# Masks, waits and one more convolution block moved between the engines of a two-model kernel

## The chip, the cores and the metric

One core of a Trainium2 chip runs the whole program. Times are device microseconds (us) of that core. Its engines are TensorE (PE in the rows; its weight loads are PEld), VectorE (DVE), ScalarE (ACT), GpSimd (POOL) and SyncE (SP), which issues the DMAs. Each takes its instructions in order and waits on semaphores.

## What is computed

Two small transformers run one after the other on 256 tokens of width 1024, batch 1, in float32. Cut to what matters here:

```python
# block 1, layer 0: convolution module; layer 1: forgetting attention over 12 heads
def conformer_conv(u, b_glu, w_dw, b_dw, ln_g, ln_b):
    a, gate = jnp.split(u + b_glu, 2, axis=-1)
    v = a * jax.nn.sigmoid(gate)
    v = causal_dwconv(v, w_dw, b_dw)          # 31 taps, 768 channels, one filter a channel
    return jax.nn.silu(layernorm(v, ln_g, ln_b))
# both layers: 4 heads of attention to a memory, then
x = x + jnp.concatenate([mix, mem_o], axis=-1) @ w_out[l]
x = x + conv_ffn(rmsnorm(x, g_ffn[l]), w_up[l], w_dw_f[l], b_dw_f[l], w_down[l])

# block 2, layer 1: sparse attention, 16 heads; for each of the two blocks of 128 queries
p_c = softmax over 16 compressed keys, p_s over selected keys, p_w over a window
return gates[..., 0:1] * o_c + gates[..., 1:2] * o_s + gates[..., 2:3] * o_w
```

With 256 tokens there are four selection blocks, and all are selected, so p_s and p_w are both causal attention over the keys, with different keys.

## The kernel before, in words

**Weights.** They come as 173 tiles of 1 MB (`TILES`), always in the same order. SP loads tile t into one of three slots of `RAW`, after VectorE is through with tile t-3. ScalarE rounds it to `WH` (line 1318), VectorE subtracts and writes the rest to `WL` (line 1687), and TensorE takes three products for each pair: high by high, low by high, high by low (lines 792 to 794). ScalarE may round tile t only when TensorE has used tile t-3 (`w_used`). On ScalarE and VectorE the place of these two instructions in the queue is written by hand: `upto(key)` or `upto_n(n)` rounds (or splits) all tiles up to n+2 that are not done yet.

**The convolution** works on six blocks of 128 channels. Four (`PE_BLOCKS` = 2, 3, 4, 5) are matmuls on TensorE (line 944): the sequence is copied by DMA into four shifted copies (`shift(j)` on SP, 16 DMAs each, for a pair of blocks), and the taps are diagonal matrices of 32 by 32, which GpSimd builds from `pick` and the tap values (line 724). Blocks 0 and 1 are done on VectorE, 31 taps each, one instruction a tap (lines 1880 and 1882), in turn, spread over the program by `taps(count)`. TensorE's blocks lie in the slots of the first memory attention (`CONV_SLOTS`). The mean for the layer norm (line 1090) needs all six.

**Attention** runs as a pipeline of slots. In slot s TensorE takes a piece of a weight tile, the scores of head s, the transposes of head s-2 and, for every second slot, the product with the values. VectorE takes the maximum (line 1793), ScalarE the exponential (line 1403), VectorE normalizes (line 1779) and copies the transposes (line 1801). In the second attention (12 heads and 4 memory heads, `base` 4) `FOX_PIECES` says which tile's half goes to which slot; slot 11 ends `("qm", 1)`, whose bank VectorE empties with `by_head` (line 1758), and slots 12 to 16 hold halves of `("o1", c)`.

**The FFN** runs 11 steps (`ffn`); step s has the tiles fg and fv, and from step 2 (`LAG`) also fd of step s-2. ScalarE does the middle tap (line 1424), the tanh (line 1428, which waits for VectorE) and the high part of the product (line 1433); VectorE does the scaling (line 1748), two taps (lines 1830, 1834) and the low part.

**A normalized input** is transposed by TensorE (line 926), and ScalarE writes the high parts from the bank (line 1351), VectorE the low parts (line 1716). Norm 3 has two gains, hence two targets: `KH`/`KL` (in MH/ML) first needed by tile `("k1", 0)`, and `XH`/`XL`.

**The sparse attention** has 16 heads, one in a slot. In slot s TensorE computes the scores of head s into two banks, `Ss` and `Sw` (lines 1262 to 1269), then the transposes of head s-1 (lines 1275, 1276), one whole tile of queries or gates (48 matmuls), and the values of head s-1 (lines 1290 to 1293). Masks are added on TensorE: matmuls of an identity in bf16 with the masks `causb` and `cmpb`. VectorE takes five maxima from the banks (lines 2250 to 2254); ScalarE reads the banks again for the six exponentials (line 1652), copies a transposed part (lines 1662, 1663) and then rounds the next tile; VectorE normalizes (line 2282) and splits the tile.

## Time and profile before

| | |
|---|---|
| median of 3 runs | 1224.46 us (1223.63 to 1225.26) |
| the profiled execution | 1224.42 us |
| its span, first to last instruction | 1222.6 us |
| PE busy | 1176.3 us, 96% of the span |
| DVE busy | 854.8 us, 70% |
| ACT busy | 599.6 us, 49% |
| mean granted TensorE clock | 0.990 |

Busy PE is the time in which a matmul is in flight, so it hides what a matmul costs; the spacing of starts shows that. A wait row names an engine's first instruction behind the wait and who released it. The granted clock is 1.0 at 2.4 GHz and 0.5 at 1.2 GHz.

### The profile page before, as it was taken

Reading aid. Unit: us, or ns where it says so; the run is one execution under the profiler, and the core shown is the slowest. Engines: PE = TensorE matmul, PEld = TensorE weight load, DVE = VectorE, ACT = ScalarE, POOL = GpSimd, SP = SyncE. Lnnn points to the kernel's source line nnn. Section 1 sums busy time; section 2 is a strip of 40 time slices with the busy share of each in tenths; the row PEclk is TensorE's granted clock in tenths of the full one; section 3 lists DMA queues with packets and bytes.
Section 4 is the critical chain, followed back from the end, with each engine's and each line's share of the span. In section 5 each row is a group of like instructions: output and inputs, shape, how many; then the busy total and the mean of one; then the engine's idle time right before and its main releaser. Section 6 shows DMA issues by size and latency. Waiting matters only on the chain.

```text
span 1222.6 us, 19215 instructions
## 1 busy us (share of the span) xinstructions
PE 1176.3 (96%) x7966; PEld 1054.6 (86%) x7966; DVE 854.8 (70%) x1310; ACT 599.6 (49%) x933; POOL 24.6 (2%) x40
## 2 busy tenths in 40 slices
PE   6989998999999999899999999999999999999997
PEld 6958898999899779899999978878799789999885
DVE  5995678787767657887778856665676257777664
ACT  6525545545554435455545334444553245565552
POOL 3000000000000000000000000000000000000000
PEclk9999999999999999999999999999999999999998
DMA  9634444555443314455544544544575522322351
GB/s 378 209 108 158 173 173 174 199 179 179 183 173 118 125 69 173 140 205 177 198 176 152 208 158 149 203 156 155 206 276 207 211 99 99 106 103 104 136 192 50
DMA packets 31398, 202.81 MB, mean 166 GB/s; under 512 B 4048, under 2 KB 4176, under 8 KB 8784
## 3 DMA queue, kind: packets, MB, share of 16 engines
q1 hardware_dynamic: 31312, 201.58, 45.3%
q8 instruction: 63, 1.03, 0.3%
q14 instruction: 23, 0.19, 0.0%
HBM read 198.18 MB, written 1.05 MB: 163 GB/s over the span
## 4 chain that ended last, share of the span: by engine, by line
PE 82%; DVE 9%; ACT 4%; issue 2%; DMA 1%; DVEq 0%; ACTq 0%; POOLq 0%; SPq 0%; POOL 0%
PE bank L792 24%; PE bank L793 23%; PE bank L794 23%; DVE WL L1687 3%; ACT WH L1318 2%; DVE work L1882 2%; PE bank L1292 1%; PE bank L1275 1%; PE bank L1218 1%; PE bank L1182 1%; PE bank L926 1%; PE bank L1006 1%; DMA xn<-cmpw 1%; PE bank L1266 1%; DVE work L1834 1%
## 5 line engine op out<-in xcount | busy, mean ns | idle before, releaser
L1687 DVE TENSOR_TENSOR WL<-RAW,WH 128x2048 fp32r<-128x2048 f32 x172 | 394.8, 2298 | 154.4 <-ACT WH L1318 153.2
L1318 ACT ACTIVATE WH<-RAW 128x2048 fp32r<-128x2048 f32 x172 | 328.5, 1912 | 215.5 <-PE bank L794 207.6
L792 PE MATMUL bank<-XH,WH 128*128 128x256 f32 x1264 | 363.1, 287 | 19.5 <-DVE WL L1903 11.9
L793 PE MATMUL bank<-XL,WH 128*128 128x256 f32 x1264 | 359.5, 284 | 0.0
L794 PE MATMUL bank<-XH,WL 128*128 128x256 f32 x1264 | 359.4, 284 | 0.0
L792 PEld LDWEIGHTS bank<-XH,WH 128*128 128x128 f32 x1264 | 244.4, 193 | 23.6 <-DVE XL L1896 11.8
L793 PEld LDWEIGHTS bank<-XL,WH 128*128 128x128 f32 x1264 | 244.5, 193 | 0.6
L794 PEld LDWEIGHTS bank<-XH,WL 128*128 128x128 f32 x1264 | 244.3, 193 | 0.0
L792 PE MATMUL bank<-WH,MH 128*128 128x512 f32 (+1 forms) x480 | 182.3, 380 | 3.7 <-DVE work L1758 2.7
L793 PE MATMUL bank<-WL,MH 128*128 128x512 f32 (+1 forms) x480 | 179.9, 375 | 0.0
L794 PE MATMUL bank<-WH,ML 128*128 128x512 f32 (+1 forms) x480 | 179.5, 374 | 0.0
L792 PEld LDWEIGHTS bank<-WH,MH 128*128 128x128 f32 x480 | 91.1, 190 | 20.9 <-DVE work L1758 2.9
L794 PEld LDWEIGHTS bank<-WH,ML 128*128 128x128 f32 x480 | 91.2, 190 | 16.2
L793 PEld LDWEIGHTS bank<-WL,MH 128*128 128x128 f32 x480 | 91.3, 190 | 14.7 <-issue 0.2
L792 PE MATMUL bank<-WH,XH 128*128 128x512 f32 x192 | 76.3, 397 | 0.0
L794 PE MATMUL bank<-WH,XL 128*128 128x512 f32 x192 | 74.8, 389 | 0.0
L793 PE MATMUL bank<-WL,XH 128*128 128x512 f32 x192 | 74.7, 389 | 0.0
L792 PE MATMUL bank<-MH,WH 128*128 128x256 f32 x208 | 60.2, 289 | 5.9 <-DVE ML L1716 2.9
L793 PE MATMUL bank<-ML,WH 128*128 128x256 f32 x208 | 58.8, 283 | 0.0
L794 PE MATMUL bank<-MH,WL 128*128 128x256 f32 x208 | 58.8, 283 | 0.0
L1652 ACT ACTIVATE work<-bank,stat,rs_n 128x128 f32<-128x128 f32 (+2 forms) x96 | 43.0, 463 | 23.7 <-DVE stat L2256 23.7
L1424 ACT ACTIVATE work<-work,par 128x256 f32<-128x256 f32 x88 | 47.5, 588 | 6.3 <-DVE work L1748 6.3
(294 smaller groups left out, 1471.3 us busy)
## 6 DMA issues: line engine op xcount, KB each, us to landing
RAW<-wstream SPq DMA_DIRECT2D x173, 1024.0 KB, 4.8
con<-cmpw SPq DMA_DIRECT2D x6, 512.0 KB, 5.7
xn<-cmpw SPq DMA_DIRECT2D x4, 512.0 KB, 7.6
con<-consts SPq DMA_DIRECT2D x1, 1617.0 KB, 6.7
work<-xT_in SPq DMA_DIRECT2D x1, 1024.0 KB, 4.9
x<-x_in SPq DMA_DIRECT2D x1, 1024.0 KB, 10.8
work<-mem_in SPq DMA_DIRECT2D x1, 1024.0 KB, 15.8
xn<-memT_in SPq DMA_DIRECT2D x1, 1024.0 KB, 13.2
```

The lines of the kernel that those rows point to most:

```text
L792: mm(o, ah, bh, start=start, stop=False)
L793: mm(o, ah, bl, start=False, stop=False)
L794: return mm(o, al, bh, start=False, stop=stop)
L926: last = nc.tensor.transpose(o[j][:, kk * T + i * P:kk * T + (i + 1) * P], x[:, i, (2 * j + kk) * P:(2 * j + kk + 1) * P], ident)
L1006: mm(o[:, a:a + n], q1[h % 2][:, h // 2, t], k1[:, h // 2, 0:n], start=True, stop=False)
L1182: last = mm(o[:, :], sdt[:, h % 2, a:a + P], rv[:, m, :], start=(m == 0), stop=(m == i))
L1218: last = mm(o_cmp[r, 0:256], blocks[:, l, r], cmp_w[n % 2][2 * v + i // 4][:, c], start=(n == 0 and i == 0), stop=(n == 3 and i == 7))
L1318: act_fn(WH[:, t % RING, :], RAW[:, t % RING, :], ACT.Copy).then_inc(w_rounded, 1)
L1424: act_fn(fy[:, e, c], fu[:, e, c], ACT.Identity, bias=col(f"b_dw_f{l}", f), scale=col(f"w_dw_f{l}", 2 * 44 + f)).then_inc(act_for_dve, 1)
L1652: ins = act_fn((pC, pS, pW)[dst][:, e, b:b + w], B((name, s))[:, a:a + w], ACT.Exp, bias=stat[:, c:c + 1], scale=rs_n[:, i:i + 1], accum_o ...
L1687: tt(WL[:, t % RING, :], RAW[:, t % RING, :], WH[:, t % RING, :].bitcast(F32), ALU.subtract).then_inc(w_split, 1)
L1882: link(stt(conv[:, b, :], vpad[:, b, i - 1:i - 1 + T], tap(b, i - 1), conv[:, b, :], ALU.mult, ALU.add))
```

## The change

Six things at once.

- **FFN.** For the first two steps both engines had one tile more in their `upto_n` (the term `0 < 2 * s + q < 2 * LAG`). It is gone. ScalarE now rounds one tile before the tanh in steps 0, 1 and 2.
- **Second attention.** `by_head(("qm", 1), ...)` moves on VectorE from the end of slot 11 to ahead of that slot's maximum; VectorE's `upto` in slot 16 is left out there and comes behind the loop.
- **Norm 3.** ScalarE and VectorE do both pairs of the first gain before the second gain. ScalarE waits for VectorE's low part of a pair before it reads the bank for the second gain.
- **Sparse slots.** No mask matmuls. The key array is laid out anew, so that four score matmuls (144, 272, 256 and 128 columns) do what four of 256, 256, 272 and 16 did. VectorE adds the masks and takes the maxima in one instruction a segment, six in a slot, each followed by a read of the accumulator, and writes the masked scores to SBUF; ScalarE takes the exponentials there. The banks `Ss` and `Sw` are freed by VectorE. Tiles are rounded and split a slot earlier. ScalarE's copy of the transposed part comes ahead of its exponentials. From slot 13 on VectorE's `output` comes at the end of a slot for the head before.
- **Convolution.** Block 1 goes to TensorE too; VectorE keeps block 0, with half as many taps at each place.
- **Tap matrices and shifts.** The diagonal matrices come from DRAM ready made (512 KB a block, 5 DMAs behind the loads of tiles 5 to 8) and GpSimd builds none. Each group of 16 shift DMAs stands behind one more weight load than before, and there is a third, shorter group for block 1.

```diff
-PE_BLOCKS = (2, 3, 4, 5)
+PE_BLOCKS = (2, 3, 1, 4, 5)
-CONV_SLOTS = {0: [(2, 0), (2, 1)], 1: [(3, 0)], 2: [(3, 1)], 3: [(4, 0)], 4: [(4, 1)], 5: [(5, 0)], 6: [(5, 1)]}
+CONV_SLOTS = {0: [(2, 0), (2, 1)], 1: [(3, 0)], 2: [(3, 1), (1, 0)], 3: [(1, 1)], 4: [(4, 0), (4, 1)], 5: [(5, 0)], 6: [(5, 1)]}
+TAPS_AFTER = {5: (2, 3), 6: (1,), 7: (4,), 8: (5,)}
...
-                if TILES[t] == ("mk", 1):
+                if TILES[t] == ("mv", 1):
                     shift(1)
                 if TILES[t] == ("o0", O0_ORDER[0]):
+                    shift(0)
+                if TILES[t] == ("o0", O0_ORDER[1]):
                     sp.wait_ge(w_used, TILE[("qm", 0)] + 1)
                     shift(2)
...
                 load(t)
+                for b in TAPS_AFTER.get(t, ()):
+                    if t == 5:
+                        sp.wait_ge(front_lo, KD)
+                    sp.dma_start(conv_w[b], tapw[b].rearrange("p (n c) -> p n c", c=DIAG)).then_inc(conv_w_loaded[b], 16)
...
-            conv_weights(2)
-            conv_weights(3)
-            conv_weights(4)
             rms(0)
-            conv_weights(5)
...
-                    mm(oS[:, 0:T], q0, k[:, P:P + T], start=True, stop=False)
-                    mm(oS[:, 0:T], identb[:, :], causb[:, :], start=False, stop=True)
-                    mm(oS[:, T:2 * T], q1_, k[:, 0:T], start=True, stop=False)
-                    mm(oS[:, T:T + P], identb[:, :], causb[:, 0:P], start=False, stop=True).then_inc(aux_done, 1)
-                    mm(oW[:, 0:T + CMP_S], q1_, k[:, T:KALL], start=True, stop=False)
-                    mm(oW[:, P:T], identb[:, :], causb[:, 0:P], start=False, stop=False)
-                    mm(oW[:, T + CMP_S:T + 2 * CMP_S], q0, k[:, 2 * T:KALL], start=False, stop=False)
-                    mm(oW[:, T:T + 2 * CMP_S], identb[:, :], cmpb[:, :], start=False, stop=True).then_inc(aux_done, 1)
+                    at = P + CMP_S
+                    mm(oS[:, 0:at], q0, k[:, P:T + CMP_S], start=True, stop=False)
+                    mm(oS[:, at:at + T + CMP_S], q1_, k[:, 0:T + CMP_S], start=False, stop=True).then_inc(aux_done, 1)
+                    mm(oW[:, 0:T], q1_, k[:, KEYS_WIN], start=True, stop=False)
+                    mm(oW[:, T:T + P], q0, k[:, at + P:at + 2 * P], start=False, stop=True).then_inc(aux_done, 1)
...
-                for j in (2 * h, 2 * h + 1):
-                    ready(act, ("tr", n, j))
-                    for dst, _, name in [norms[n][g] for g in gains]:
+                for at, (dst, _, name) in enumerate([norms[n][g] for g in gains]):
+                    for j in (2 * h, 2 * h + 1):
+                        ready(act, ("tr", n, j))
+                        if at:
+                            act.wait_ge(part_done, j + 1)
...
-                        upto_n(at + 1 + q + (0 < 2 * s + q < 2 * LAG))
+                        upto_n(at + 1 + q)
...
                         if q == 0:
+                            if s <= LAG:
+                                upto_n(at + 2)
                             act.wait_ge(*dve_a.next())
...
-                    if s in pieces:
+                    if s in pieces and s < n:
                         upto(pieces[s][0])
+                    if s in pieces and pieces[s] == (("qm", 1), 1):
+                        by_head(("qm", 1), q_mem)
...
-                    link(nc.vector.tensor_reduce(m3[:, 1:3, 0], oS[:, 0:T].rearrange("p (b k) -> p b k", b=2), AX_X, ALU.max))
-                    link(nc.vector.tensor_reduce(mx[:, 3:4], oS[:, T:2 * T], AX_X, ALU.max))
-                    link(nc.vector.tensor_reduce(mx[:, 0:1], oW[:, T + CMP_S:T + 2 * CMP_S], AX_X, ALU.max))
-                    link(nc.vector.tensor_reduce(mx[:, 1:2], oW[:, T:T + CMP_S], AX_X, ALU.max))
-                    link(nc.vector.tensor_reduce(mx[:, 5:6], oW[:, 0:T], AX_X, ALU.max))
+                    for br, i, dst, b, w, name, a, mask in NSA_SEGMENTS:
+                        ins = nc.vector.tensor_tensor_reduce((pC, pS, pW)[dst][:, e, b:b + w], B((name, s))[:, a:a + w], mask, 1.0, -3e38,
+                                                             ALU.add, ALU.max, mx[:, 2 * br + i:2 * br + i + 1])
```

**ScalarE in the third step of an FFN.** Before, from the high part of step 1 to the first tap of step 2's second half:

```order
L1433 ACTIVATE MH<-work 128x512 [waits dve_for_act]
L1424 ACTIVATE work<-work,par 128x256 [waits freed_A_dve]
L1424 ACTIVATE work<-work,par 128x256
L1428 ACTIVATE work<-work 128x512 [waits dve_for_act]
L1318 ACTIVATE WH<-RAW 128x2048 [waits w_used,w_loaded2]
```

Now (line 1430 was 1433, 1311 was 1318, 1425 was 1428):

```order
L1430 ACTIVATE MH<-work 128x512 [waits dve_for_act]
L1311 ACTIVATE WH<-RAW 128x2048 [waits w_used,w_loaded1]
L1419 ACTIVATE work<-work,par 128x256 [waits freed_A_dve]
L1419 ACTIVATE work<-work,par 128x256
L1311 ACTIVATE WH<-RAW 128x2048 [waits w_used,w_loaded2]
L1425 ACTIVATE work<-work 128x512 [waits dve_for_act]
```

The tile of slot 2 (fv of step 3) is rounded ahead of the tanh and its wait for VectorE, and the tile of slot 1 came to stand in this step instead of the one before.

**TensorE and VectorE in a slot of the sparse attention.** Before, TensorE's scores with the first transpose behind them, and VectorE's maxima with the output ahead of them:

```order
L1262 MATMUL bank<-work 128x256 [waits freed_A_act,freed_B_act]
L1263 MATMUL bank<-causb,identb 128x256
L1264 MATMUL bank<-work 128x256
L1265 MATMUL bank<-causb,identb 128x128
L1266 MATMUL bank<-work 128x272
L1267 MATMUL bank<-causb,identb 128x128
L1268 MATMUL bank<-work 128x16
L1269 MATMUL bank<-cmpb,identb 128x32
L1275 MATMUL bank<-ident,work 128x128 [waits prob_done,freed_A_dve,freed_A_act]
```

```order
L2241 SCALAR_TENSOR_TENSOR xn<-bank,work 128x256 [waits aux_done]
L2250 TENSOR_REDUCE stat<-bank 128x2 [waits freed_B_dve,aux_done]
L2251 TENSOR_REDUCE stat<-bank 128x1
L2252 TENSOR_REDUCE stat<-bank 128x1
L2253 TENSOR_REDUCE stat<-bank 128x1
L2254 TENSOR_REDUCE stat<-bank 128x1
L2256 SCALAR_TENSOR_TENSOR stat<-stat,rs_n 128x6 [waits dve_chain]
```

Now the same on TensorE, and the first rows on VectorE (ISA is the fused instruction, ISA stat the read of its accumulator):

```order
L1259 MATMUL bank<-work 128x144 [waits freed_A_act,freed_B_dve]
L1260 MATMUL bank<-work 128x272
L1261 MATMUL bank<-work 128x256
L1262 MATMUL bank<-work 128x128
L1268 MATMUL bank<-ident,work 128x128 [waits prob_done,freed_A_dve,freed_A_act]
```

```order
L2234 SCALAR_TENSOR_TENSOR xn<-bank,work 128x256 [waits aux_done]
L2249 ISA work,stat<-bank,con 128x128 [waits freed_B_dve,aux_done]
L2249 ISA stat 128x1
L2249 ISA work,stat<-bank,con 128x16
L2249 ISA stat 128x1
L2249 ISA work,stat<-bank,con 128x256
```

Four matmuls left TensorE's slot, and five instructions of VectorE became twelve (six pairs).

**SP's queue around the shifts.** Before, where the first 16 shift DMAs begin, and now:

```order
L642 DMA xn<-memT_in 128x2048
L619 DMA RAW<-wstream 128x2048 [waits w_split] x5
L627 DMA MH<-work 32x572 [waits glu_done]
```

```order
L682 DMA work<-tapw 128x1024 [waits front_lo]
L682 DMA gfree<-tapw 128x1024 [waits front_lo]
L626 DMA RAW<-wstream 128x2048 [waits w_split]
L682 DMA con<-tapw 128x1024
L626 DMA RAW<-wstream 128x2048 [waits w_split]
L682 DMA con<-tapw 128x1024
L626 DMA RAW<-wstream 128x2048 [waits w_split]
L682 DMA con<-tapw 128x1024
L626 DMA RAW<-wstream 128x2048 [waits w_split]
L638 DMA MH<-work 32x572 [waits glu_done]
```

Tile 9 is loaded ahead of the shifts instead of behind them, and five tap matrices stand between the loads of tiles 5 to 9.

## Rows read from the trace of the kernel before

**Rows 1.** The page, busy time of the engines with instruction counts:

```profile
PE 1176.3 (96%) x7966; PEld 1054.6 (86%) x7966; DVE 854.8 (70%) x1310; ACT 599.6 (49%) x933; POOL 24.6 (2%) x40
```

**Rows 2.** TensorE's waits, whole run: line, releaser, total us, times, longest:

```profile
PE bank L792 <- DVE WL L1687: 8.8, 6, 3.3
PE bank L1017 <- DVEq L1802: 3.9, 2, 2.6
PE bank L792 <- DVE ML L1716: 2.9, 3, 1.5
PE bank L792 <- DVE work L1758: 2.7, 1, 2.7
PE bank L1275 <- DVE work L2282: 1.0, 1, 1.0
```

**Rows 3.** Busy time by stretch, last columns: clock, DMA share, GB/s:

```profile
90.00:93.40 3.40, 2.93 (x20) 1.42 (x24) 2.92 (x8) 3.23 (x7) 0.00 (x0) 0.51 0.00 0
...
192.40:195.80 3.40, 3.40 (x30) 3.40 (x30) 3.40 (x4) 2.43 (x3) 0.00 (x0) 0.99 0.36 113
...
509.90:513.30 3.40, 3.31 (x15) 3.35 (x16) 3.33 (x7) 0.79 (x2) 0.00 (x0) 0.50 0.67 236
```

**Rows 4.** Timeline, first FFN, third step: start, us, engine, instruction, idle before:

```profile
184.12 0.63 ACT L1428 ACTIVATE work<-work 128x512 f32<-128x512 f32 x1 [1.98 <-DVEq L1837]
184.66 1.90 ACT L1318 ACTIVATE WH<-RAW 128x2048 fp32r<-128x2048 f32 x1
...
186.59 2.29 DVE L1687 TENSOR_TENSOR WL<-RAW,WH 128x2048 fp32r<-128x2048 f32 x1 [1.72 <-ACT WH L1318]
```

**Rows 5.** Timeline, end of the second attention, VectorE and TensorE:

```profile
420.13 0.47 PE L792 MATMUL bank<-WH,MH 128*128 128x512 f32 x1 [2.69 <-DVE work L1758]
...
443.13 2.29 DVE L1687 TENSOR_TENSOR WL<-RAW,WH 128x2048 fp32r<-128x2048 f32 x1 [0.98 <-ACT WH L1318]
...
447.33 0.44 PE L1017 MATMUL bank<-work,mvv 128*64 128x256 f32 x2 [2.57 <-DVEq L1802]
```

**Rows 6.** TensorE's waits from 20 to 130 us:

```profile
PE bank L792 <- issue: 2.1, 1, 2.1
PE bank L979 <- DVE work L1779: 2.0, 2, 1.2
PE bank L1017 <- DVEq L1802: 1.4, 1, 1.4
PE bank L792 <- DVE WL L1687: 1.3, 2, 1.0
```

**Rows 7.** The chain that ended last, half a convolution block; then VectorE's taps, timeline:

```profile
95.40 1.86 PE bank L944 x32
...
57.27 3.26 DVE L1882 SCALAR_TENSOR_TENSOR work<-work,par 128x256 f32<-128x256 f32 x8
```

**Rows 8.** Timeline, TensorE in one sparse slot: first score, mask, transpose, next slot:

```profile
1006.24 0.60 PE L1262 MATMUL bank<-work 128*128 128x256 f32 x2
1006.68 0.27 PE L1263 MATMUL bank<-causb,identb 128*128 128x256 bf16 x1
...
1008.07 0.31 PE L1275 MATMUL bank<-ident,work 128*128 128x128 f32 x1
...
1016.48 0.38 PE L1262 MATMUL bank<-work 128*128 128x256 f32 x1
```

**Rows 9.** Groups of VectorE, 1006 to 1120 us: count, busy, mean ns, idle before:

```profile
L1687 DVE TENSOR_TENSOR WL<-RAW,WH 128x2048 fp32r<-128x2048 f32 x12 | 27.5, 2292 | 7.1 <-ACT WH L1318 7.1
...
L2250 DVE TENSOR_REDUCE stat<-bank 128x2 f32<-128x256 f32 x11 | 4.7, 426 | 7.9 <-PE bank L1269 7.9
...
L2252 DVE TENSOR_REDUCE stat<-bank 128x1 f32<-128x16 f32 x11 | 1.8, 165 | 0.0
```

**Rows 10.** Timeline, VectorE in one sparse slot: bias, then behind the exponentials:

```profile
1030.00 0.17 DVE L2256 SCALAR_TENSOR_TENSOR stat<-stat,rs_n 128x6 f32<-128x6 f32 x1
...
1033.01 0.19 DVE L2271 RECIPROCAL stat<-stat 128x6 f32<-128x6 f32 x1 [1.14 <-ACT work L1652]
```

More of the change, by code:

```diff
@@ L1709, in low @@
             def low(n, h, gains=(0,)):
-                for j in (2 * h, 2 * h + 1):
-                    dve.wait_ge(*hi_a.next(2 * len(gains)))
-                    for g in gains:
-                        hi, dst, name = norms[n][g]
+                for g in gains:
+                    hi, dst, name = norms[n][g]
+                    for j in (2 * h, 2 * h + 1):
+                        dve.wait_ge(*hi_a.next(2))
                         for kk in range(2):
@@ L1863, in ple @@
                         low(8, 0)
-            TAPS_IN_SLOT = 4
-            dve_taps = [(b, i) for i in range(CONV) for b in (0, 1)]
+            TAPS_IN_SLOT = 2
+            dve_taps = [(0, i) for i in range(CONV)]
             n_tap, last_of, glu_at = [0], {}, {}
@@ L1934, in _ @@
                             .then_inc(front_lo, 1)
-                taps(6 if j < 2 else 8)
+                taps(3)
             dve.wait_ge(mask_made, 1)
@@ L1938, in _ @@
             upto(("qm", 0))
-            taps(10)
+            taps(5)
             spread(0)
@@ L1942, in _ @@
             upto(("mk", 0))
-            taps(8)
+            taps(6)
             upto(("mv", 0))
@@ L2229, in gate_in, with output @@
                 scaled(("ng", t), nu.rearrange("p (b t) -> p b t", b=2))
+            upto(("ng", 0))
             gate_in(0)
             gate(0)
-            upto(("ng", 0))
+            EARLY_OUT = NSA_H - 3
+            def output(h):
+                e = h % 2
+                ready(dve, ("On", h))
+                free(stt(om[:, e, :], B(("On", h))[:, 0:T], 0.5, gs[:, (h // 2) % 2, e * T:e * T + T], ALU.mult, ALU.mult),
+                     ("On", h), "dve")
+                is_free(dve, ("On", h))
+                dve.drain().then_inc(dve_for_act, 1)
@@ L2234, in _ @@
             for s in range(NSA_H + 2):
                 e = s % 2
[L2236 to L2244 removed]
+                if 2 <= s <= EARLY_OUT:
+                    output(s - 2)
@@ L2392, in param_array, with conv_tap_matrices @@
     return np.ascontiguousarray(np.concatenate([v[n] for n, _ in PARAM_PARTS], axis=1))
-def conv_taps_by_shift(w):
-    out = np.zeros((SHIFTS * STEPS, 4 * P), np.float32)
-    out[0:CONV] = w[:, 2 * P:]
-    return out.reshape(STEPS, SHIFTS, 4, GROUPS, DIAG).transpose(1, 4, 2, 3, 0).reshape(P, 4 * GROUPS * STEPS)
+def conv_tap_matrices(w):
+    taps = np.zeros((SHIFTS * STEPS, MIX), np.float32)
+    taps[0:CONV] = w
+    taps = taps.reshape(STEPS, SHIFTS, NMB, GROUPS, DIAG).transpose(2, 1, 4, 3, 0).reshape(NMB, P, GROUPS * STEPS)
+    out = np.zeros((NMB, P, GROUPS * STEPS, DIAG), np.float32)
+    for r in range(P):
+        out[:, r, :, r % DIAG] = taps[:, r]
+    return out.reshape(NMB, P, GROUPS * STEPS * DIAG)
 def channels(v):
```

147 lines of the change are left out of this document (69 added, 78 removed).

## Prediction

> **What bounds the kernel now.** I read the page's busy times first: a matmul is in flight for 96% of the span [rows 1]. That share says only that TensorE is the engine to watch, not that it runs at its peak, so the second view is its waits [rows 2]: few and short, some 23 us beside the start of the run, which nothing here touches [rows 2, 6]. They come in clusters: two of 3.3 us in the FFNs, 2.7 and 2.6 at the end of the second attention, and 6.8 in four entries in the convolution [rows 2, 6]. The third view is the granted clock by stretch [rows 3]. Behind five of the waits it is at 0.5 (1.2 GHz) for 3.4 us: from 90.0, 189.0, 421.1, 448.4 and 509.9; rows 3 show the first and the last. In such a stretch TensorE starts 15 or 16 matmuls of a gemm, in the next one of the same length 30. So each costs another 3.4 / 2 = 1.7 us, and removing a wait of 3 us pays 5. Everywhere else TensorE runs back to back, and there only fewer or shorter matmuls help. The sparse slots are such a place: of rows 2 only the 1.0 us lies there, in the second slot, and from then on it is VectorE that waits for TensorE, by 7.9 / 11 = 0.7 us a slot [rows 9].
>
> **FFN, both of them.** The wait of 3.3 us is for the low part of tile fv of step 3 [rows 2]. The split begins at 186.59, after VectorE stood 1.72 us for ScalarE, whose rounding ran at 184.66 because it is queued behind the tanh of 184.12, itself held 1.98 us by VectorE [rows 4]. ScalarE did not wait for TensorE or a load before it, so data and slot were there. It is a knot of two queues and no shortage. The change puts the rounding ahead of the tanh: it would run in the 1.98 us idle from 182.1, ready at 184.0. That alone moves the split 2.6 us. The same 1.72 us wait stood in each of the two steps before, and the surplus tile of step 0 kept VectorE a whole split, 2.3 us, from its taps, so VectorE also arrives earlier. Laid out instruction by instruction with the durations of rows 4 (rounding 1.90, split 2.29), I get the split done at about 182 instead of 188.9. TensorE wants it at 188.9 - 3.3 = 185.6: a margin of some 3.5 us. The tile before it (fg of step 3) is the next to be late: split done near 177.4, wanted a tile earlier, at about 179.8 (48 matmuls at 0.12 us), a margin of 2.3. Next in line is therefore TensorE itself. Gain 3.3 + 1.7 = 5.0 each, 10.0 for both; if the margins were all wrong, 0, if half a wait stays and the clock still falls, 3.
>
> **Second attention.** The 2.69 us at 420.13 are for `by_head` of tile qm [rows 5], since `("o1", 0)` needs its bank. In the new place VectorE starts it about when TensorE ends that tile, and it is out 0.3 us after TensorE wants the bank. What is queued behind it is the maximum of slot 11, late by some 0.5 us; nobody waits, for the probabilities of slot 11 are wanted two slots later. Gain 2.4 + 1.7. The 2.57 us at 447.33 come behind a split of 2.29 us that VectorE did ahead of the copy [rows 5]. Without it the copy starts when the transpose is there, and 0.68 + 0.2 us of copy and drain stay: gain 1.7 + 1.7. The split then comes behind the loop; its tile is wanted some 8 us later, so it is free. Together 7.5; bounds 4 (clock falls all the same) and 8.5.
>
> **Norm 3.** TensorE waits 2.9 us in three places for line 1716 [rows 2], the longest (1.5) at norm 8, which keeps its order, the other 1.4 at tile ("k1", 0). With the first gain done first, VectorE's low part starts two ScalarE instructions (0.7 us) earlier and the second pair follows at once. Gain 1.3, at least 0.5. ScalarE's new wait for VectorE is about 0.2 us per pair, under TensorE's transposes.
>
> **Convolution.** Removed from VectorE: 31 taps of block 1. In the rows a tap of alternating blocks costs 3.26 / 8 = 0.4 us [rows 7]. With one block each tap waits for the one before; I take 0.5. So VectorE does 31 x 0.5 = 16 us where it did 62 x 0.4 = 25: 9 us less before 98 us, where its taps stood ahead of the scaling and splits that TensorE waited for. Added on TensorE: a block is two halves of 1.86 us [rows 7], 3.7 us on the path. Tile 9's load no longer stands behind 16 shift DMAs. Played through, the waits of 6.8 us and one half-clock stretch (1.5) go, as VectorE is 2 to 4 us early at each: 6.8 + 1.5 - 3.7 = 4.6, of which I take 4.5. In my laying out of SP's queue the shifts for block 4 leave by 75 us and are wanted at 82, those for block 1 by 64 and are wanted at 76. The tap matrices are 2.6 MB more, half a megabyte beside each megabyte tile. At one tile in 5.7 us that is 184 + 92 = 276 GB/s; 236 GB/s made the DMA engines 0.67 busy [rows 3], so they fit. GpSimd's building is off every path. Bounds: 6, and -2 if half the waits stay and 3.7 is paid.
>
> **Sparse slots.** The first matmul of a slot to the next slot's is 1016.48 - 1006.24 = 10.24 us, and scores with masks take 1008.07 - 1006.24 = 1.83 [rows 8]. A score of 256 columns takes 0.44 [rows 8]. Before and after there are 800 columns of scores, so without masks they take at best 800 / 256 x 0.44 = 1.38: gain 0.45. At the least it is what the masks' 544 columns cost at the gemm's pace of 3.4 us / 30 for 256 columns [rows 3]: 0.24. I take 0.40, because the two 16-column pieces, costly for their size, vanish into wider ones. 16 slots: 6.4; bounds 3.8 and 7.2. TensorE's 1.0 us wait for line 2282 in slot 1 [rows 2] goes as well, since the rounding and split of the tile move ahead of slot 0. Sum 7.4.
>
> This holds only if VectorE's loop fits into 9.84 us. Before it took 10.24 - 0.72 = 9.52 [rows 8, 9]. The columns are again 800. Added are one instruction and six reads of an accumulator, which no row of VectorE shows. The nearest are its 16-column maxima, spaced 0.08, and ScalarE's read of its accumulator at 0.2: seven short instructions are 0.6 to 1.4 us. The exponentials (3.0 us, [rows 10]) read SBUF instead of a bank; from 0.0 to 0.3. The 7.1 / 12 = 0.6 us wait for ScalarE's rounding [rows 9] goes, as its copy no longer stands in front. 9.52 + 0.6 + 0.1 - 0.6 = 9.6 fits; with the high ends 10.6 does not. I take the low one, since spacing on the same engine is the nearer row. A little over would not hurt either: by the same laying out the probabilities are ready about 2.5 us before TensorE wants them, so a loop 0.2 us too long is used up only after 12 slots.
>
> **Sum.** 10.0 + 7.5 + 1.3 + 4.5 + 7.4 = 30.7. The profiled execution took 1224.42 us with a span of 1222.6; the median is 1224.46, so what lies around the span stays 1.8 and the same sum holds for both: 1224.46 - 30.7 = 1193.8.
>
> **Rivals.**
> *The slot becomes VectorE's.* If the accumulator reads cost 0.2, the loop is 10.2 to 10.6; after the 2.5 us of reserve the slots run at that pace, 0.0 to 0.4 over the old one for some eight of them. The sparse gain falls from 7.4 to between 0 and 4: 1197 to 1201. Against it: short instructions on VectorE are spaced 0.08.
> *The fused instruction runs at half pace.* It has a bank and SBUF as sources and an accumulator. At two cycles a column the 800 columns add 800 / 256 x 0.33 = 1.0 us: a loop of 10.6 from the third slot on, sparse -5 instead of +7.4: about 1206. Against it: a tap, which reads two f32 tensors from SBUF without an accumulator, keeps 0.4 us for 256 columns [rows 7]. The Trainium skill, "Vector Engine (DVE) Microarchitecture Reference", section "Points that are easy to get wrong", says that this family of instructions halves its throughput with two non-bf16 SBUF sources, since no port is left for the accumulator. By its letter a bank as one source escapes it, and the taps of this trace don't show it; if it applied here too, the time would be this rival's.
> *The queues knot again elsewhere.* One of the FFN margins (2.3 us) or of the attention's is wrong by more than itself, and as the code is the same in both FFNs it costs twice: 6 to 10 us less gain, 1199 to 1204.
> *The convolution does not pay.* Shifts or VectorE's chain in the memory attention hold TensorE, and 3.7 us are paid for nothing: 1198 to 1200.
> *Slower than before.* Only the fused instruction can do it: with 23 us gained elsewhere, 13 slots would each have to be 1.9 us longer than 10.24, a loop of 12.1. That needs 0.7 us for each of the six pairs on average, where I count 0.3: an instruction that falls off its normal path, as one without a name of its own in this list could. About 1230.
>
> **Chances.** Forecast 0.55, VectorE's slot 0.13, half pace 0.06, a knot 0.10, convolution 0.07, slower 0.03, more gain than the sum (down to 1187, all upper bounds) 0.06. The range 1187 to 1203 takes in all but the last cases of half pace, knot and slower. A change within 0.2% (2.4 us), which is about what a measurement can tell, would need one case to eat exactly the rest: 0.01. Faster 0.96.
>
> **What would show it.** Right: TensorE's waits in both FFNs' third steps gone and no stretch at 0.5 before the last microseconds; scores from first matmul to transpose in 1.4 us and slots of 9.84; the last half block of the convolution (95.4 before, [rows 7]) at about 91; line 1716's wait at k1 about 0.1. Wrong: TensorE waiting in the sparse slots for the normalization on VectorE (rival one or two, told apart by the spacing of the fused instructions: 0.35 or 0.6 for 256 columns, and by that of the reads), waits for shifts or tap matrices at line 944, or a gap in the FFN that moved to another tile.

## The result, and the profile after

The changed kernel takes 1193.95 us (median of four runs, 1192.96 to 1194.86), the kernel before 1224.86 us in the same measurement: a ratio of 0.975, 95% interval 0.973 to 0.977. The prediction was 1193.8. It hit, but as a sum whose terms erred in both directions; where each erred is shown below. The profiled execution took 1194.86 us with a span of 1193.1.

The page after, busy time of the engines:

```profile
PE 1163.9 (98%) x7966; PEld 1049.0 (88%) x7966; DVE 842.8 (71%) x1392; ACT 604.9 (51%) x934; POOL 14.2 (1%) x33
```

TensorE's waits after, whole run (line, releaser: total us, times, longest); they answer to [rows 2]:

```profile
PE bank L789 <- DVE WL L1897: 12.2, 1, 12.2
PE bank L789 <- DVE ML L1710: 1.5, 1, 1.5
PE bank L789 <- issue: 1.1, 1, 1.1
PE bank L1013 <- DVEq L1798: 1.0, 1, 1.0
PE bank L789 <- DVE WL L1681: 1.0, 2, 0.7
PE bank L1214 <- DMA xn<-cmpw: 0.9, 1, 0.9
PE bank L789 <- DVE work L1752: 0.6, 1, 0.6
```

The first is the start of the run; the one of 1.1 us, to which the profile gives no releaser ("issue"), stands in norm 3 and is taken up below. Of the 8.8 us for splits 1.0 is left, and both FFNs and the whole convolution have no wait at all. Busy time by stretch, in the places where the clock had fallen or would fall (us, busy and instructions of PE, PEld, DVE, ACT, POOL; clock, DMA share, GB/s); it answers to [rows 3]:

```profile
90.00:93.40 3.40, 3.40 (x55) 1.75 (x48) 1.77 (x2) 0.00 (x0) 0.00 (x0) 1.00 0.00 0
177.00:180.40 3.40, 3.40 (x31) 3.40 (x30) 3.37 (x6) 2.17 (x2) 0.00 (x0) 1.00 0.48 142
408.50:411.90 3.40, 3.13 (x14) 2.67 (x15) 1.79 (x7) 2.72 (x5) 0.00 (x0) 1.00 0.00 0
433.00:436.40 3.40, 3.40 (x19) 2.52 (x18) 2.00 (x2) 0.39 (x1) 0.00 (x0) 1.00 0.00 0
```

All at 1.0, and the trace records no fall of the clock between 18.3 and 1189.0 us; the kernel before had five. The two spans differ by 29.5 us. Read at the same instruction in both traces, they part as in the table. The instructions are TensorE's: the first spreading of a norm (the matmuls with `rstd` at line 839 before, 836 now), then the first transposes of norms 2, 3, 4 and 6, the first sparse score, and the first transposes of the last norm.

| stretch | lead gained, us | predicted |
|---|---|---|
| start, to the first spreading (21.93 before, 23.56 after) | -1.6 | 0 |
| convolution, to norm 2 | 5.6 | 4.5 |
| first FFN, to norm 3 | 5.0 | 5.0 |
| norm 3, to its spreading | 0.45 | 1.3 |
| second attention, to norm 4 | 6.7 | 7.5 |
| second FFN | 4.9 | 5.0 |
| block 2 up to the sparse scores | -0.5 | 0 |
| sparse slots | 9.0 | 7.4 |

The medians differ by 30.9: this execution was the slowest of its four, 0.9 us over their median, and the profiled one before was 0.4 under its own. The first line of the table is taken up at the end.

### The profile page after: what moved, and what is told of

It reads as the page before. It is cut to its first block, busy times and chain, and to the rows that moved or that the text cites. A ratio compares the mean times of both kernels' runs of the same rounds, so it can differ in the third digit from the quotient of the medians.

```text
span 1193.1 us, 19344 instructions
## 1 busy us (share of the span) xinstructions
PE 1163.9 (98%) x7966; PEld 1049.0 (88%) x7966; DVE 842.8 (71%) x1392; ACT 604.9 (51%) x934; POOL 14.2 (1%) x33
## 4 chain that ended last, share of the span: by engine, by line
PE 93%; DVE 3%; ACT 1%; DMA 1%; issue 1%; SPq 0%; DVEq 0%; POOLq 0%; POOL 0%; ACTq 0%
PE bank L789 27%; PE bank L790 26%; PE bank L791 26%; PE bank L940 2%; PE bank L1285 1%; DVE WL L1681 1%; PE bank L1214 1%; PE bank L1178 1%; PE bank L923 1%; PE bank L1268 1%; DMA xn<-cmpw 1%; PE bank L994 1%; PE bank L1002 1%; PE bank L1260 1%; PE bank L975 1%
## 5 line engine op out<-in xcount | busy, mean ns | idle before, releaser
L1657 ACT ACTIVATE work<-work,stat,rs_n 128x128 f32<-128x128 f32 (+1 forms) x96 | 46.6, 487 | 14.4 <-DVE stat L2258 14.4
L1742 DVE TENSOR_TENSOR work<-bank,rb 128x512 f32<-128x512 f32 x59 | 40.7, 689 | 12.4 <-PE bank L791 9.1
```

Source lines behind the costliest of these rows:

```text
L1657: ins = act_fn(score, score, ACT.Exp, bias=stat[:, c:c + 1], scale=rs_n[:, i:i + 1], accum_out=stat[:, 16 + c:17 + c])
L1742: ins = tt(dst, src, rbb, ALU.mult)
```

## Experiments: each part undone alone

Each run below is the changed kernel with one part put back as it was, or in two cases a piece of one. Together the five whole parts cost 29.2 us when undone one at a time (10.1, 4.9, 0.4, 4.2 and 9.6), close to the 30.9 of the change, so the parts depend little on each other.

**The FFN part.**

```diff
-                        upto_n(at + 1 + q)
+                        upto_n(at + 1 + q + (0 < 2 * s + q < 2 * LAG))
...
-                            if s <= LAG:
-                                upto_n(at + 2)
```

> The changed kernel with the FFN part alone undone: both engines have their surplus tile in the first two steps again, and ScalarE rounds no tile ahead of the tanh. Theory A (the parts add up, and the half clock behind a wait belongs to its price): TensorE waits 3.3 us again in the third step of each FFN, with a stretch at a granted clock of 0.5 behind it, and each FFN is 5.0 us longer; 1193.95 + 9.9 = 1203.9. Rival B (the clock fell in the kernel before because of what lay around the waits, not because of this wait): only 3.3 us each, 1200.6, and no stretch at 0.5. Rival C (in the new kernel VectorE reaches the FFN earlier, so part of the wait is gone anyway): under 3 us each, below 1200.

Measured: 1204.03 us, 10.1 more than the changed kernel. TensorE waits 3.26 us at 184.76 and 3.25 at 498.59, and behind the first of them:

```profile
184.70:188.10 3.40, 3.34 (x17) 3.38 (x18) 3.33 (x7) 0.79 (x2) 0.00 (x0) 0.58 0.62 222
```

Theory A. The mean clock of this window is 0.58, because the half-clock stretch starts half a microsecond into it (185.2 to 188.6). In it 15 spacings stand at 0.213 us instead of 0.12, which is 1.4 us. The second wait has such a stretch from 499.3 on. All four executions had a mean clock of 0.993 or 0.994 (0.997 or 0.998 in the changed kernel), so behind these waits it fell in all four.

**Half of the FFN part.** The surplus tile stays away, but nothing is rounded ahead of the tanh.

```diff
-                            if s <= LAG:
-                                upto_n(at + 2)
```

> The changed kernel with half of the FFN part undone: the surplus tile stays away, but ScalarE rounds no tile ahead of the tanh. The prediction gave the rounding ahead of the tanh 2.6 us of the 6.9 by which the split moved. Theory A (the knot is the rounding queued behind the tanh): the split of the tile fv in step 3 comes some 2.6 us or more later than in the changed kernel, the wait is back, and as no tile is rounded early at all, other tiles of the first steps are late too; 1203 or more. Rival B (the surplus tile made the delay by holding VectorE from its taps for 2.3 us): without it the order of rounding and tanh doesn't matter, 1194 to 1195.

Measured: 1198.57 us, 4.6 more: neither theory. TensorE's waits in the first FFN, then two stretches of it:

```profile
PE bank L789 <- DVE WL L1679: 2.0, 2, 1.4
```

```profile
176.00:179.40 3.40, 3.38 (x28) 3.40 (x29) 2.23 (x5) 1.74 (x2) 0.00 (x0) 1.00 0.60 241
179.40:182.80 3.40, 2.83 (x24) 2.66 (x23) 2.68 (x2) 3.40 (x4) 0.00 (x0) 1.00 0.16 67
```

Undoing the early rounding costs 2.4 us an FFN, and putting the surplus tile back on top of that another 2.6 (the run before). No run has the surplus tile together with the early rounding, so this split of the gain holds for this order only. Without the surplus tile the wait of 3.3 is down to 1.4 and 0.6 us, and behind 1.4 the clock stays at 1.0, in both FFNs. The stage from norm 2 to norm 3 is 2.43 us longer for listed waits of 1.98: a wait costs about 0.2 us more than its row says. A matmul is in flight for 0.28 us and starts every 0.12, and the row counts from the end of the flight, which explains 0.16 of it.

**The second attention.**

```diff
-                    if s in pieces and s < n:
+                    if s in pieces:
                         upto(pieces[s][0])
-                    if s in pieces and pieces[s] == (("qm", 1), 1):
-                        by_head(("qm", 1), q_mem)
...
+                        elif name == "qm":
+                            by_head((name, j), q_mem)
```

> The changed kernel with the part on the second attention alone undone: by_head for tile qm at the end of slot 11, and VectorE's split ahead of the copy in slot 16. Theory A: TensorE waits 2.7 us for by_head and 2.6 for the copy, as before, each with a stretch at a granted clock of 0.5 behind it; by the stages of the two traces 6.7 us, 1200.6. Rival B (the second FFN takes some of it back, since VectorE comes to it earlier or later): the wait in the attention returns in full, but the end moves by less than 5 us.

Measured: 1198.83 us, 4.9 more, the four executions from 1197.77 to 1200.28. In the profiled one, the slowest, both waits are back (2.70 and 2.57) and the attention is 6.6 us longer. Behind them:

```profile
410.20:413.60 3.40, 3.34 (x9) 2.72 (x10) 2.64 (x3) 0.43 (x1) 0.00 (x0) 0.55 0.00 0
437.60:441.00 3.40, 3.40 (x13) 2.04 (x10) 0.43 (x1) 0.38 (x1) 0.00 (x0) 0.57 0.56 236
```

The mean clock was 0.994 in this execution and 0.997, 0.996 and 0.997 in the other three; 0.997 is too high for two stretches. The waits alone make 3.6 us (1197.6), with both stretches 6.6 (1200.5): the same two waits, 2.6 and 2.7 us in the profiled execution, drop the clock twice in one execution and at most once in another. In the kernel before it was 0.989 to 0.991 in every execution on record. So the 1.7 us that the prediction gave each of these two waits were there in that kernel, but are no property of the waits alone.

**Norm 3.**

```diff
-                for g in gains:
-                    hi, dst, name = norms[n][g]
-                    for j in (2 * h, 2 * h + 1):
-                        dve.wait_ge(*hi_a.next(2))
+                for j in (2 * h, 2 * h + 1):
+                    dve.wait_ge(*hi_a.next(2 * len(gains)))
+                    for g in gains:
+                        hi, dst, name = norms[n][g]
```

(and the same in ScalarE's `high`)

> The changed kernel with the part on norm 3 alone undone. Theory A (read off the two traces: 1.24 us gained at the first half of the norm, 0.79 given back at the second, where TensorE now waits for VectorE's split of the next tile): the waits of 0.85 and 0.53 us for the low part return, the one of 1.09 behind the second transposes shrinks to 0.33, and the time is 0.45 us longer, 1194.4, which only the trace can tell. Rival B (the prediction's figure of 1.3 was right and the 1.09 us wait has another origin, such as the earlier arrival of the stage): 1195.3, and the wait of 1.09 stays.

Measured: 1194.38 us, 0.4 more, which is less than the runs of one kernel differ, so the trace decides. It has two waits of 0.85 and 0.53 us for the low part and one of 0.33 behind the second transposes. Theory A. The stretch from the first transposes to the spreading is 14.18 us, and 13.73 in the changed kernel.

**The convolution.** The whole part back, from the number of blocks to GpSimd's tap matrices:

```diff
-PE_BLOCKS = (2, 3, 1, 4, 5)
+PE_BLOCKS = (2, 3, 4, 5)
...
-            TAPS_IN_SLOT = 2
-            dve_taps = [(0, i) for i in range(CONV)]
+            TAPS_IN_SLOT = 4
+            dve_taps = [(b, i) for i in range(CONV) for b in (0, 1)]
```

> The changed kernel with the convolution part alone undone: four blocks on TensorE, two on VectorE, tap matrices built by GpSimd, shifts where they were. Theory A: waits of 6.7 us in the convolution and one stretch at a granted clock of 0.5 return, and two half blocks of 1.86 us leave TensorE; by the stages of the two traces, counted from the first spreading of a norm, 5.6 us, 1199.5. Rival B (what the trace puts down to the convolution is partly the start of the run, where the first matmuls ran at half pace for 6 us in one profile and for 3 in the other): 4 us, 1198.

Measured: 1198.14 us, 4.2 more; three executions at 1198.0 to 1198.2, the profiled one at 1199.9. TensorE's waits there, from 20 to 130 us:

```profile
PE bank L797 <- issue: 2.1, 1, 2.1
PE bank L984 <- DVE work L1782: 1.7, 2, 1.2
PE bank L1022 <- DVEq L1807: 1.4, 1, 1.4
```

Behind the 2.1 us at 57.6 the clock is at 0.5 for 3.4 us, which it was not in the kernel before behind the same wait; a second stretch, from 91.8, stands where the kernel before had its one. From the first spreading to norm 2 it takes 114.2 us, and 108.4 in the changed kernel: 5.8, of which the stretch at 57.6 is about 1.5. Theory A for the trace, B's figure for the median. The mean clock was 0.997 in two of the three faster executions and 0.996 in the profiled one, which fits one stretch less in those two; only the slowest has a trace, so this is not shown.

**Only the place of the shifts.** Five blocks on TensorE, but two groups of shifts a weight load earlier.

```diff
-                if TILES[t] == ("mv", 1):
+                if TILES[t] == ("mk", 1):
                     shift(1)
...
                     shift(0)
-                if TILES[t] == ("o0", O0_ORDER[1]):
```

> The changed kernel with the shift DMAs of blocks 2 and 3 and of blocks 4 and 5 one weight load earlier again, all else as changed (five blocks on TensorE, tap matrices from DRAM). Theory A (the wait of 2.07 us at 56.73 in the kernel before came from SP's queue: tile 9's load stood behind 16 shift DMAs, which wait for the gated values): a wait of 1 to 2 us is back near 56 us, and the time is 1 to 2.5 us longer, 1195 to 1196.5. Rival B (it came from VectorE's taps, of which only half are left): nothing returns, 1194.

Measured: 1193.39 us, no wait of TensorE from 20 to 130 us, and again 108.4 us from the first spreading to norm 2. Rival B: the place of the shifts does nothing for the time here. What removed the waits is then among the things that the run before put back together: VectorE's taps, the block on TensorE and GpSimd's matrices. The traces point to the taps. Before, six of them (48.50, 2.46 us) stand ahead of the scaling that ScalarE waits for, and the split that TensorE needs ends at 56.6; in the changed kernel three stand there (47.78, 1.52 us) and the split ends at 55.0. No run has the taps apart from the rest.

**The sparse slots.** All of that part back, here its core:

```diff
-                    mm(oS[:, 0:at], q0, k[:, P:T + CMP_S], start=True, stop=False)
+                    mm(oS[:, 0:T], q0, k[:, P:P + T], start=True, stop=False)
+                    mm(oS[:, 0:T], identb[:, :], causb[:, :], start=False, stop=True)
...
-                    for br, i, dst, b, w, name, a, mask in NSA_SEGMENTS:
-                        ins = nc.vector.tensor_tensor_reduce(...)
+                    link(nc.vector.tensor_reduce(mx[:, 3:4], oS[:, T:2 * T], AX_X, ALU.max))
```

> The changed kernel with the sparse part alone undone: masks by matmul, maxima from the banks, exponentials from the banks, tiles split a slot later. Theory A: slots of 10.24 us instead of 9.73, 16 of them, and the wait of 1.0 us in slot 1: 9.0 us by the stages of the two traces, 1203.0. The prediction had 7.4, 1201.4. What tells them apart is the spacing of slots, 0.51 or 0.40 longer.

Measured: 1203.57 us, 9.6 more; slots of 10.23 us where the changed kernel has 9.73, and the wait of 1.0 us in slot 1 is back. Theory A.

## Experiments: what a sparse slot costs

**The masks alone, on top.**

```diff
                     mm(oS[:, 0:at], q0, k[:, P:T + CMP_S], start=True, stop=False)
+                    mm(oS[:, 0:P], identb[:, :], causb[:, 0:P], start=False, stop=False)
```

(one such matmul behind each of the four scores)

> The changed kernel with four mask matmuls in bf16 put back on TensorE in each sparse slot, one behind each score (4 x 128 = 512 columns), beside the masks that VectorE adds; the mask is thus added twice, which changes no probability. It prices the masks alone, without the narrow pieces of the old layout. Theory A (they cost the 0.24 us that their spacing shows and nothing more): slots of 9.97, 16 x 0.24 = 3.8 us, 1197.8. Theory B (each change between bf16 and float32 costs the matmul behind it some 0.02 to 0.06 on top, which the 272 column score at 0.52 before and 0.46 now hints at): slots of 10.03 to 10.1, 4.8 to 6 us, 1198.8 to 1200. Rival C: the slot is already VectorE's, and TensorE's surplus is hidden: under 1196.

Measured: 1198.96 us, 5.0 more, slots of 10.11: 0.39 us a slot, and 5.9 us for the sparse stage in the traces. The changed kernel's scores first, then this kernel's (start, us, engine, line, operation); the spacing of the starts is what a matmul costs:

```profile
983.53 0.41 PE L1259 MATMUL bank<-work 128*128 128x144 f32 x2
983.78 0.62 PE L1260 MATMUL bank<-work 128*128 128x272 f32 x2
984.24 0.59 PE L1261 MATMUL bank<-work 128*128 128x256 f32 x2
984.67 0.38 PE L1262 MATMUL bank<-work 128*128 128x128 f32 x2
984.89 0.49 PE L1268 MATMUL bank<-ident,work 128*128 128x128 f32 x3
```

```profile
983.57 0.65 PE L1263 MATMUL bank<-work 128*128 128x256 f32 x2
984.05 0.22 PE L1264 MATMUL bank<-causb,identb 128*128 128x128 bf16 x1
984.11 0.44 PE L1265 MATMUL bank<-work 128*128 128x128 f32 x2
984.39 0.22 PE L1266 MATMUL bank<-causb,identb 128*128 128x128 bf16 x1
984.44 0.50 PE L1272 MATMUL bank<-ident,work 128*128 128x128 f32 x3
```

A mask takes 0.055 us, but the 128 column score behind one takes 0.28 where it takes 0.22 alone, and the 256 column score 0.48 instead of 0.43. Four masks are 0.22 us by their own rows and 0.39 by the slot. That is theory B's figure, but not its reason. In the kernel before, one mask has 256 columns and the others fewer:

```profile
1006.78 0.60 PE L1264 MATMUL bank<-work 128*128 128x256 f32 x2
1007.22 0.22 PE L1265 MATMUL bank<-causb,identb 128*128 128x128 bf16 x1
1007.22 0.30 PEld L1266 LDWEIGHTS bank<-work 128*128 128x128 f32 x2
1007.27 0.68 PE L1266 MATMUL bank<-work 128*128 128x272 f32 x2
1007.79 0.22 PE L1267 MATMUL bank<-causb,identb 128*128 128x128 bf16 x1
```

The score at 1006.78 stands behind the 256 column mask in bf16 and takes its usual 0.44; the one at 1007.27 stands behind the 128 column mask and takes 0.52, where the changed kernel's of 272 columns takes 0.46. The type changes in both places, so the change of type isn't the reason. What fits these rows is the weight load: two float32 loads in a row start 0.11 us apart (two of 0.19 us fill 0.30 in the row of L1266), a mask of 256 columns lasts as long (0.109), and one of 128 columns (0.055) leaves the other half of it open. This is read from the rows; no run was made for it.

**One more instruction on VectorE in each slot.**

```diff
                 if s < NSA_H:
+                    for c in range(1):
+                        link(stt(junk[:, c * T:(c + 1) * T], x[:, 0, 0:T], 1.0, x[:, 0, T:2 * T], ALU.mult, ALU.add))
```

> The changed kernel with one more instruction on VectorE at the head of each sparse slot: a scaled addition of two 256 column pieces of SBUF, some 0.33 to 0.4 us, whose result nobody reads. VectorE's pace in the changed kernel, from the growth of its reserve (1.33 us at head 1 to 2.27 at head 13 while TensorE's slot is 9.73): 9.65 us. Its idle time of some 1.7 us a slot, for the exponentials, lies within that loop. Theory A (VectorE's own loop is the next bound, 0.08 behind TensorE): loop 10.0, the reserve of 1.3 us is gone after four to five slots, then TensorE waits and slots are 10.0: 14 x 0.3 - 1.3 = 2.5 to 3.5 us, 1196.5 to 1197.5. Rival B (the 1.7 us of idle time absorb it): nothing, 1194. The prediction's reserve of 2.5 us would give 1 to 2 us.

**Two of them**, `range(2)`.

> The same with two such instructions, 0.66 to 0.8 us a slot. Theory A: a loop of 10.3 to 10.4 us, the reserve gone after two slots, 15 x 0.65 - 1 = 8 to 9 us, 1202 to 1203. Rival B (idle time absorbs it): 1194. It also says what the rivals of the prediction would have cost, where the fused instructions or the reads of the accumulator had been slower by that much.

Measured: 1195.65 and 1200.9 us, 1.7 and 6.9 more. VectorE's period, from the first fused instruction of a slot to that of the next, mean of an even and an odd slot, is 9.61 us in the changed kernel, 9.84 with one and 10.17 with two; TensorE's slot without waits is 9.73. The reserve (from the probabilities being ready to TensorE's transpose, us) at heads 0, 1, 6 and 12 is 0.33, 1.33, 1.7 and 2.03 in the changed kernel; 0.47, 1.12, 0.37 and 0.15 with one; 0.24, 0.57, 0.15 and 0.15 with two, where 0.15 means that TensorE waits. Theory A, with 0.23 us more for the first instruction and 0.33 for the second, where two of them are spaced 0.34. The changed kernel has 0.28 us of idle time a slot ahead of the fused instructions, which can hide a part of the first. VectorE is still idle for the exponentials. The rows are of 1002 to 1100 us, ten slots (count, busy, mean ns, idle before), in the changed kernel, then with two more instructions:

```profile
L2249 DVE CUSTOM_DVE_ANT_0 work<-bank,con 128x128 f32<-128x128 f32 (+2 forms) x60 | 13.9, 293 | 2.8 <-DVE xn L2234 1.5 <-PE bank L1269 1.3
L2273 DVE RECIPROCAL stat<-stat 128x6 f32<-128x6 f32 x10 | 1.9, 192 | 17.2 <-ACT work L1657 17.2
```

```profile
L2275 DVE RECIPROCAL stat<-stat 128x6 f32<-128x6 f32 x10 | 1.9, 191 | 16.9 <-ACT work L1657 16.9
```

The 17.2 us remain 16.9 while the slots get longer: that idle time lies inside the loop (fused instruction, exponentials, normalization, split) and absorbs nothing. With two more instructions VectorE is the bound, though it is busy for 79.1 of the 98 us only, 81%.

## Experiments: two gains that were left

**Matmuls ahead of the first tile.**

```diff
+            pe.wait_ge(mask_made, 1)
+            for _ in range(34):
+                mm(bank[7][:, 0:P], ones, ones, start=True, stop=True)
             o = take(("ca", 0))
```

> The changed kernel with 34 matmuls of 128 columns in float32 on TensorE ahead of the first tile, over a constant tile, into a bank that is first used later; nobody reads them. In the ten profiles so far the first matmuls of the run ran at half pace for 2.8 to 5.8 us (spacing 0.213 us instead of 0.12), which costs 1.4 to 2.9 us, and differs from execution to execution of one kernel. Theory A (TensorE starts at the low level of its clock because it did nothing for 12 us): the half pace falls into the idle time before the first tile; gain 1.4 to 2.9 us, 1191.0 to 1192.5, and the spread of the runs (1.9 us over four) gets smaller. Rival B (what holds the first matmuls back is tied to the first tile: loads of weights, or the other engines' start): no gain.

Measured: 1191.81 us, 2.1 less, with a spread of 0.9 instead of 1.9. From 14.9 to 18.3 us in the changed kernel, then here:

```profile
14.90:18.30 3.40, 3.40 (x18) 3.40 (x18) 2.27 (x2) 3.40 (x9) 0.71 (x1) 1.00 1.00 401
```

```profile
14.90:18.30 3.40, 3.40 (x31) 3.40 (x30) 2.03 (x2) 3.40 (x9) 0.70 (x1) 1.00 0.99 397
```

18 matmuls against 31. The view prints a granted clock of 1.00 in both, but only because the trace has no record of the clock that early: its first one, a rise to full speed, comes at 18.25 us in the changed kernel and at 5.88 here. The spacing of 0.213 us ends there too, in the changed kernel at 18.3. Theory A.

**The same, and norm 3's split earlier.** Only where a norm has two gains, VectorE's `add(acc, 3)` and `upto(key)` go between the first and the second gain:

```diff
                 for g in gains:
+                    if g and between:
+                        between()
                     hi, dst, name = norms[n][g]
```

> The same warm-up, and at norm 3 VectorE's last addition to the residual and its split of the next tile moved from behind the second gain's low part to ahead of it. Theory A (TensorE's 1.09 us wait behind the second transposes is for that split, which stands behind four low parts and an addition): the wait goes, 0.8 to 1.0 us, and the low part of the second gain is still in time; 0.9 us less than with the warm-up alone. Rival B (the second gain's low part, now 2.9 us later, is late instead): the wait moves to the tile q1 and nothing is gained. The trace tells, since 0.9 us is hardly more than the runs differ.

Measured: 1190.32 us (1189.74 to 1190.39), ratio 0.972, 95% interval 0.970 to 0.973, 3.6 less than the changed kernel: the fastest version here. VectorE at norm 3 in the changed kernel (the split ends at 329.08, and TensorE goes on at 329.18 after its wait of 1.09 us), then here, then TensorE's wait there:

```profile
326.20 0.68 DVE L1697 TENSOR_TENSOR x<-bank,x 128x512 f32<-128x512 f32 x1
326.80 2.28 DVE L1681 TENSOR_TENSOR WL<-RAW,WH 128x2048 fp32r<-128x2048 f32 x1
```

```profile
321.44 0.68 DVE L1700 TENSOR_TENSOR x<-bank,x 128x512 f32<-128x512 f32 x1
322.04 2.28 DVE L1684 TENSOR_TENSOR WL<-RAW,WH 128x2048 fp32r<-128x2048 f32 x1
324.24 1.65 DVE L1715 SCALAR_TENSOR_TENSOR XL<-bank,par,XH 128x256 fp32r<-128x256 f32 x4
```

```profile
PE bank L789 <- DVE XL L1715: 0.4, 1, 0.4
```

The 1.09 us wait is 0.39 now, for the second gain's low part: a little of rival B, but the stage is 1.0 us shorter than with the warm-up alone. Theory A. The medians differ by 1.5; in the two profiles a DMA wait ahead of the sparse stage, which no edit here touches, is 1.25 and 0.38 us.

## Why the prediction was right, step by step

**FFN, 10.0: right (9.9), for the reason given.** The split that the prediction followed ends well ahead of need. In the changed kernel it is the first of these:

```profile
176.16 2.28 DVE L1681 TENSOR_TENSOR WL<-RAW,WH 128x2048 fp32r<-128x2048 f32 x1
177.27 1.90 ACT L1311 ACTIVATE WH<-RAW 128x2048 fp32r<-128x2048 f32 x1
```

It is done at 178.44, and TensorE starts that tile without a wait at 181.66: 3.2 us, forecast 3.5. The split of the tile before it is done at 173.71, and TensorE starts that tile at 175.91, 2.2 us later; forecast 2.3. The prediction gave 2.6 of the split's 6.9 us to the early rounding and left the surplus tile as a further help; the second experiment shows that leaving out the surplus tile is not enough. Whether the early rounding alone would be was not run. And 3.3 + 1.7 was right as a sum of two errors: it is 3.26 + 0.2 for the flight of the last matmul + about 1.5 for the spacings at half clock.

**Second attention, 7.5: the mechanism right, the size 6.7.** The term mis-sized is what stays: 0.61 us for `by_head` where 0.3 was taken, 1.04 for the copy where 0.88 was, and twice 1.5 instead of 1.7 for the clock. What the working did not see is that the clock's share hangs on the execution (the run with this part undone).

**Norm 3, 1.3: the step that failed is that nothing was named as late next.** The two waits at the first half of the norm went as worked out: the lead grows from 8.94 us at the first transposes to 10.18 at the second (337.21 before, 327.03 after). Then VectorE's split of the next tile, queued behind four low parts and an addition, takes 0.79 back. 0.45 is left, even under the bound of 0.5.

**Convolution, 4.5: 5.6.** The added block cost its 3.7 us (halves at 77.04 and 80.38, 1.84 and 1.87), and one block's taps start 0.52 us apart on VectorE, forecast 0.5 (0.40 for two blocks in turn). All waits went; the last half block starts at 91.4, forecast 91. The term that was too small is the waits: six of them with 0.2 us each on top of the listed 6.7. That tile 9's load no longer stands behind 16 shift DMAs was right and worth nothing. No wait for shifts or tap matrices: that rival fell.

**Sparse slots, 7.4: 9.0.** The scores take 1.36 us (forecast 1.4), but the slot lost 0.50 us instead of 0.40. By the spacings in both traces, 0.25 are the masks themselves, 0.09 what the float32 matmuls behind them were late by, the first transpose among them, and the remaining 0.16 the narrow pieces. The mis-sized step is the 0.40, a value picked between bounds, and its upper bound of 0.45 was too low as well. The loop on VectorE was forecast at 9.6 and is 9.61. The two bets that decided this hold, read at 1025 us (start, us, operation):

```profile
1025.69 0.42 DVE L2249 CUSTOM_DVE_ANT_0 work<-bank,con 128x256 f32<-128x256 f32 x1
1026.04 0.08 DVE L2249 DVE_READ_ACCUMULATOR2_ANT stat<- 128x1 f32 x1
1026.04 0.17 DVE L2249 CUSTOM_DVE_ANT_0 work<-bank,con 128x16 f32<-128x16 f32 x1
1026.13 0.08 DVE L2249 DVE_READ_ACCUMULATOR2_ANT stat<- 128x1 f32 x1
```

The fused instruction over 256 columns is spaced 0.35 us, full pace, and the read of the accumulator starts with the next fused instruction and adds nothing to the spacing. So the rival of half pace fell. The Trainium skill ("Vector Engine (DVE) Microarchitecture Reference", "Points that are easy to get wrong") has the throughput halved for two non-bf16 sources in SBUF. Here one of the two is a bank, and 0.35 us for 256 columns agrees with that. The instructions added above do have two float32 sources in SBUF, without an accumulator, and are spaced 0.34, not halved. No run has two sources in SBUF with an accumulator. The rival of VectorE's slot also fell, but by 0.12 us: the reserve was put at 2.5 us and is 0.3 to 2.3, and the runs with more instructions on VectorE show what it would have cost: 1.7 us for a loop 0.11 over TensorE's, 6.9 for 0.44 over. The prediction's 1197 to 1201 for reads of 0.2 us each was too mild: it stood for loops of 10.2 to 10.6, and one of 10.17 already takes 1200.9.

**What was outside the sum:** -1.6 us at the start and -0.5 ahead of the sparse stage, most of it a DMA that TensorE waits 0.91 us for instead of 0.49. Together with 0.9 and 0.8 too much at norm 3 and in the attention they ate what convolution and sparse slots gave beyond the forecast (1.1 and 1.6), and the traces part by 1.2 us less than the 30.7 of the sum. The medians part by 0.2 more, since the two profiled executions lie on opposite sides of their medians. The hit to 0.2 us was luck within a range that was earned.

## To carry to other kernels

Price a wait of TensorE as its row plus what is hidden in the flight of the matmul before it (here 0.2 us), and the clock's share as an extra. It came every time behind 3.3 us, came and went behind 2.1 to 2.7, and was absent behind a single wait of 1.4, but not behind three shorter ones close together (below). When a reordering on one engine removes a wait, walk its queue on to the next thing TensorE needs from it: at norm 3 that was the split of the next tile, and moving it too was worth more than the edit itself. And before counting on an engine's idle time, ask whether it lies inside a loop with another engine: 1.7 us a slot of it absorbed nothing.

## What the runs showed of the chip that was not expected

- The first matmuls of a run are spaced 0.213 us instead of 0.12 for a while that differs between executions: 2.8 us in the profile of before, 5.8 in that of after, 3.2 to 5.8 in those of the first ten experiments. In each of these twelve profiles the trace's first record of the clock, a rise to full speed, lies within 0.15 us of the place where the spacing shrinks (14.94 us before, 18.25 after). It is 1.2 to 2.5 us of the time. Matmuls on a constant in the idle time before remove it, and the spread of one kernel's four runs went from 1.9 to 0.9 us. Another part that differs is the DMA wait ahead of the sparse stage, 0.3 to 1.3 us in these profiles. The Trainium skill ("TensorE: Matmul & The Clock Gate", "What's actually happening") has the slow start, with a point of transition that varies by half a microsecond either way; here it lay 3.1 to 6.2 us behind the first matmul.
- The same wait (2.07 us near 57 us) was followed by a stretch at half clock in one profile and by none in another; a group of three shorter waits, 0.8, 1.2 and 1.4 us within 9 us, had such a stretch begin in its last one, at 90.0, in the kernel before; with the convolution part undone, a group of 0.5, 1.2 and 1.4 had one from 91.8.
- A mask matmul of 128 columns between float32 scores costs more than its own spacing: 0.055 us by its rows, 0.10 by what the slot gains without it. One of 256 columns does not.
